# A hand-ordered fast-matrix-product kernel: the third role cast after the next set's second, and the openings and seams put in another order

## The reference

```python
def swiglu(x, w_gate, w_up, w_down):
    return (jax.nn.silu(x @ w_gate) * (x @ w_up)) @ w_down
...
for l in range(2):
    if l == 1: ...                      # shared K, V and log-forget rows from rms_norm(x, g_kv_b)
    x = x + 0.5 * swiglu(rms_norm(x, g_norm[l, 0]), ...)      # D_FF = 2816
    ...                                 # attention, with a cache of 512 rows
    x = x + 0.5 * swiglu(rms_norm(x, g_norm[l, 2]), ...)
y = rms_norm(x, g_final)
```

## Time and profile before

| | us |
|---|---|
| median of 3 runs | 2517.8 (2512.48 to 2520.25) |
| the profiled execution | 2516.2, span 2514.0 |
| PE busy | 2413.0 (96%) |
| DVE busy | 1859.1 (74%) |
| ACT busy | 1338.0 (53%) |
| POOL busy | 546.1 (22%) |
| mean granted TensorE clock | 0.992 of 2.4 GHz |

### The profile page before, as it was taken

One profiled execution on the slowest core, in us unless ns is written; L12 is line 12 of the kernel. 1 busy time (PEld: TensorE's weight loads), 2 busy tenths in 40 slices (PEclk: granted clock), 3 DMA queues, 4 the chain that ended last, 5 costly groups with the idle time before them and its releaser, 6 DMA issues. The chain is left out here.

```text
span 2514.0 us, 48940 instructions
## 1 busy us (share of the span) xinstructions
PE 2413.0 (96%) x18377; PEld 2267.6 (90%) x18377; DVE 1859.1 (74%) x3710; ACT 1338.0 (53%) x2870; POOL 546.1 (22%) x421
## 2 busy tenths in 40 slices
PE   8899999999998999999999999999999999999998
PEld 7899999788678999999988889999996699999998
DVE  7887979422687888787935889787928878787865
ACT  6555556201785655555622555555618856555554
POOL 0222122344000122222135122222131001222210
PEclk9999999999999999999999999999999999999999
DMA  5656565232763465756434665666457644666652
GB/s 133 122 116 139 108 139 105 88 117 85 282 241 108 93 122 112 141 119 133 94 84 138 172 130 111 138 125 129 99 210 255 224 117 78 138 116 138 124 112 82
DMA packets 419397, 334.20 MB, mean 133 GB/s; under 512 B 20641, under 2 KB 379738, under 8 KB 418914
## 3 DMA queue, kind: packets, MB, share of 16 engines
q1 hardware_dynamic: 279376, 246.98, 31.8%
q0 software_dynamic: 133136, 65.82, 21.4%
q10 hardware_dynamic: 6658, 18.37, 2.0%
HBM read 314.98 MB, written 16.13 MB: 132 GB/s over the span
## 5 line engine op out<-in xcount | busy, mean ns | idle before, releaser
L925 PE MATMUL PS<-x_area,w_area 128*128 128x320 f32 x3096 | 482.2, 309 | 0.0
L925 PEld LDWEIGHTS PS<-x_area,w_area 128*128 128x128 f32 x3096 | 461.1, 188 | 0.3 <-DVE w_area L2276 0.3
L2276 DVE TENSOR_TENSOR w_area<-R,w_area 128x512 fp32r<-128x512 f32 (+2 forms) x583 | 357.1, 617 | 119.1 <-ACT w_area L1638 118.3
L1638 ACT ACTIVATE w_area<-R 128x512 fp32r<-128x512 f32 (+2 forms) x583 | 324.8, 567 | 223.3 <-PE PS L925 88.6
L2276 DVE TENSOR_TENSOR r_area<-R,r_area 128x512 fp32r<-128x512 f32 (+2 forms) x437 | 270.6, 620 | 115.4 <-ACT r_area L1638 105.0
L925 PE MATMUL PS<-r_area,w_area 128*128 128x320 f32 x1584 | 271.2, 314 | 25.1 <-ACT PS L1723 17.1
L1638 ACT ACTIVATE r_area<-R 128x512 fp32r<-128x512 f32 (+2 forms) x437 | 248.0, 568 | 60.6 <-DVE R L2297 40.2
L925 PEld LDWEIGHTS PS<-r_area,w_area 128*128 128x128 f32 x1584 | 243.1, 191 | 32.9 <-ACT PS L1723 29.8
L1723 ACT ACTIVATE PS<-PS 128x320 f32<-128x320 f32 x438 | 179.8, 417 | 160.0 <-PE PS L925 143.7
L1148 PE MATMUL PS<-w_area,xn_hi 128*128 128x512 f32 x800 | 252.4, 397 | 4.9 <-POOL w_area L769 3.6
L925 PE MATMUL PS<-r_area 128*128 128x320 f32 x1392 | 238.4, 311 | 8.4 <-ACT PS L1723 6.0
(11 more groups left out here) (341 smaller groups left out, 4169.6 us busy)
## 6 DMA issues: line engine op xcount, KB each, us to landing
R<-in_w_ffn_up_dram SPq DMA_DIRECT2D x45, 512.0 KB, 5.3
R<-in_w_ffn_gate_dram SPq DMA_DIRECT2D x43, 512.0 KB, 5.4
R<-in_w_ffn_up_dram SPq DMA_DIRECT2D x86, 256.0 KB, 3.7
R<-in_w_ffn_up_dram POOLq DMA_DIRECT2D x86, 256.0 KB, 4.7
R<-in_w_ffn_gate_dram SPq DMA_DIRECT2D x82, 256.0 KB, 4.6
R<-in_w_ffn_gate_dram POOLq DMA_DIRECT2D x81, 256.0 KB, 4.9
R<-in_w_ffn_down_dram SPq DMA_DIRECT2D x52, 384.0 KB, 3.8
R<-in_w_ffn_down_dram SPq DMA_DIRECT2D x88, 192.0 KB, 3.2
```

What stands on the lines that cost most here:

```text
L925: last = pe.matmul(PS[:, bank, 0:HT], a[:, k, :], b, start=(start and opens), stop=(k == n - 1 and a is lo), skip_group_check=True)
L1638: act.activation(role_parts(f, g, s, role)[0], role_source(f, g, s, role), ACT.Copy).then_inc(sem("early_cast") if key in EARLY_COUNT else ...
L2276: dve.tensor_tensor(lo, role_source(f, g, s, role), hi.bitcast(F32), ALU.subtract).then_inc(sem("early_split") if key in EARLY_COUNT else ...
```

## The change

1. The third role S3(n) is cast and split after S2(n+1), no longer before S1(n+1): in `splits`, in both engines' `ffn_sets` and in both `opening_down`. PE's order of products stays.
2. In an opening, ACT does copy 1 before the high part of hidden "5" and copy 2 before the high part of S4; PE does each product of the first down set over all its blocks before the next.
3. SP issues S1's quarter of the set after next-but-one ahead of the other transfers of the set before it, which is the new order of the splits.
4. Seams: the first tiles of the projections are loaded as soon as their own raw words are free, the first hidden parts of block 0 and the store of the keys before block 2 come after the first iteration (`after_first`), and one finishing tile moves behind the next projection's first weight tile.

```diff
@@ splits
-        out += ([(then, "W11")] if then else []) + [(at, "S4")] + ([(at, "S3")] if at != order[0] else [])
-        out += ([(then, "S1"), (then, "S2")] if then else []) + [(at, "W22")] + ([(then, "W12")] if then else [])
+        out += ([(then, "W11")] if then else []) + [(at, "S4")] + ([(then, "S1"), (then, "S2")] if then else [])
+        out += ([(at, "S3")] if at != order[0] else []) + [(at, "W22")] + ([(then, "W12")] if then else [])
...
@@ SP, load_ffn
-                for g, s in chain(f):
-                    if set_at(f, g, s) is not early:
-                        quarter_load(f, g, s)
+                sets = [(f, *at) for at in chain(f) if set_at(f, *at) is not early]
+                first_quarter(*sets[0])
+                for key, then in zip(sets, sets[1:] + [None]):
+                    if then is not None:
+                        first_quarter(*then)
+                    other_quarters(*key)
...
@@ SP
             load_ffn(0)
+            load_opening_rows(w_qkv_a[0], "qkv", QKV_ORDER[0])
...
-            sp.wait_ge(stored, STORED["kt"])
+            sp.wait_ge(stored, STORED["bv"])
+            sp.wait_ge(sem("kt_stored"), 16)
...
@@ PE, opening_down
                 product(f, g, s, "W11", "1", q, True)
-                product(f, g, s, "S1", "5", v, True, (), near)
+                product(f, g, s, "S1", "5", v, True)
                 pe.wait_ge(sem("copied"), 3 * i + 1)
-                product(f, g, s, "S2", "6", q, False, (), near)
-                product(f, g, s, "W12", "2", first_rows, False, (), near)
-                product(f, g, s, "S1", "5", v, False, (), last)
-                product(f, g, s, "S2", "6", q, False, (), last)
-                product(f, g, s, "W12", "2", first_rows, False, (), last)
+                product(f, g, s, "S2", "6", q, False)
+                product(f, g, s, "W12", "2", first_rows, False)
                 pe.wait_ge(sem("copied"), 3 * i + 2)
                 product(f, g, s, "S3", "7", q, False)
...
@@ ACT, opening_down
                 hidden_rows(f, *prev, "1")
+                copy_rows(f, *cur, 1)
                 hidden_rows(f, *prev, "5")
-                copy_rows(f, *cur, 1)
                 hidden_rows(f, *prev, "7")
                 hidden_rows(f, *prev, "2")
                 role_high(f, *then, "W11")
+                copy_rows(f, *cur, 2)
                 role_high(f, *cur, "S4")
                 hidden_rows(f, *prev, "4")
+                role_high(f, *then, "S1")
+                role_high(f, *then, "S2")
                 role_high(f, *cur, "S3")
-                role_high(f, *then, "S1")
-                copy_rows(f, *cur, 2)
-                role_high(f, *then, "S2")
                 role_high(f, *cur, "W22")
...
@@ ACT, ffn_sets
                         rows_on(f, *prev, 0)
-                        role_high(f, *cur, "S3")
...
                         role_high(f, *then, "S2")
+                    if n:
+                        role_high(f, *cur, "S3")
                     role_high(f, *cur, "W22")
...
@@ DVE, opening_down
                 hidden_lows(f, *prev, "4")
-                role_low(f, *cur, "S3")
                 dve.wait_ge(w_split, SPLIT[(f, *cur, "S4")])
                 role_sum(f, *then, "S2")
                 role_low(f, *then, "S1")
                 role_low(f, *then, "S2")
                 fifth_rows(f, *cur)
+                role_low(f, *cur, "S3")
                 role_low(f, *cur, "W22")
...
@@ DVE, ffn_sets
                         hidden_sums(f, *prev, ("5", "7", "6"))
-                    if n:
-                        role_low(f, *cur, "S3")
...
                     if turned:
                         hidden_sums(f, *prev, ("4",))
                         hidden_lows(f, *prev, "7")
+                    if n:
+                        role_low(f, *cur, "S3")
                     role_low(f, *cur, "W22")
...
                         hidden_low(f, *prev, 1)
                     if after_gate and not plain:
                         gate_scaled(f, *prev, 1)
+                    if n == 0 and after_first is not None:
+                        after_first()
...
@@ DVE, ffn (the seam into a projection)
                     tile_low(name, 0)
+                    finish_one(KB - 3)
                     sums_out(f, *last)
```

More of the change, by code:

```diff
@@ L635, in load_square @@
                 base, s, first = BASE[name], SLOT[name], 0
-                if free is not None:
+                if free is None:
+                    first = 1
+                    for u in range(2):
+                        opening_tile(name, u, *cols(w, (s + u) % 2, u * P))
+                else:
                     first = 2
@@ L650, in load_square, with opening_tile, row_tile, load_opening_rows @@
                     tile(base + m * 2 + 1, 1 - s, *cols(w, 1 - s, m * 2 * P + P))
-            def load_rows(w, base, par, n_tiles, first=0):
-                with sp.Fori(0, n_tiles) as n:
+            def opening_tile(name, j, view, src):
+                sp.wait_ge(w_split, PLAN.raw_free[name, j])
+                sp.dma_start(view, src).then_inc(w_loaded[LOAD[name, j] % 2], 16)
+            def row_tile(w, s, u, at):
+                return (raw[s][:, 0:1024].rearrange("p (k m) -> p k m", k=2),
+                        w[u * 256:(u + 1) * 256, bass.ds(at, 512)].rearrange("(k p) m -> p k m", p=P))
+            def load_opening_rows(w, name, column):
+                for u in range(4):
+                    opening_tile(name, u, *row_tile(w, (SLOT[name] + u) % 2, u, column * 512))
+            def load_rows(w, base, par, n_tiles, first=0, done=0):
+                with sp.Fori(done, n_tiles) as n:
                     for u in range(4):
                         s = (par + u) % 2
-                        tile(base + n * 4 + u, s, raw[s][:, 0:1024].rearrange("p (k m) -> p k m", k=2),
-                             w[u * 256:(u + 1) * 256, bass.ds(n * 512 + first * 512, 512)].rearrange("(k p) m -> p k m", p=P))
+                        tile(base + n * 4 + u, s, *row_tile(w, s, u, n * 512 + first * 512))
             def load_attention(x, vc, f_scr):
@@ L980, in opening_down @@
             def opening_down(f, g, s):
-                i, n = PLAN.set[f, g, s], depth(g, s)
+                i = PLAN.set[f, g, s]
                 q, v, first_rows = s % 2, 2 + s % 2, 4 + s % 2
-                near, last = range(n - 1), range(n - 1, n)
                 pe.wait_ge(sem("sum_read"), i - 1)
                 product(f, g, s, "W11", "1", q, True)
-                product(f, g, s, "S1", "5", v, True, (), near)
+                product(f, g, s, "S1", "5", v, True)
                 pe.wait_ge(sem("copied"), 3 * i + 1)
-                product(f, g, s, "S2", "6", q, False, (), near)
-                product(f, g, s, "W12", "2", first_rows, False, (), near)
-                product(f, g, s, "S1", "5", v, False, (), last)
-                product(f, g, s, "S2", "6", q, False, (), last)
-                product(f, g, s, "W12", "2", first_rows, False, (), last)
+                product(f, g, s, "S2", "6", q, False)
+                product(f, g, s, "W12", "2", first_rows, False)
                 pe.wait_ge(sem("copied"), 3 * i + 2)
@@ L1842, in ffn_sets, with ffn @@
                         finish_one(tiles)
-                        finish_one(tiles + 1)
+                        if then is not None:
+                            finish_one(tiles + 1)
                 copy_rows(f, *order[-1], 3)
-            def ffn(f, mean=None, finish_one=None, name=None):
-                ffn_sets(f, mean, finish_one)
+            def ffn(f, mean=None, finish_one=None, name=None, after_first=None):
+                ffn_sets(f, mean, finish_one, after_first)
                 if name is not None:
-                    for k in range(2):
-                        tile_high(name, k)
-                        finish_one(KB - 2 + k)
+                    tile_high(name, 0)
+                    finish_one(KB - 3)
+                    tile_high(name, 1)
+                    for k in range(KB - 2, KB):
+                        finish_one(k)
                     return
@@ L2125, in _, with first_hidden_casts @@
             x_highs("4")
-            for part in HIDDEN_PARTS[1:]:
-                first_hidden_cast(part)
-            ffn(0, None, partial(finish_tile, 0, 0, 0, 1), "qkv")
+            def first_hidden_casts():
+                for part in HIDDEN_PARTS[1:]:
+                    first_hidden_cast(part)
+            ffn(0, None, partial(finish_tile, 0, 0, 0, 1), "qkv", first_hidden_casts)
             act.wait_ge(w_used, BASE["qkv"])
@@ L2139, in _ @@
             act.wait_ge(sem("lam_sums"), 2)
-            act.activation(small[:, 4:6], small[:, 6:8], ACT.Exp).then_inc(sem("lam_exps"), 1)
+            act.activation(small[:, 4:6], small[:, 6:8], ACT.Exp).then_inc(sem("small_exps"), 1)
             act.preload_act_table_set("natural_log_exp_and_others")
@@ L2166, in _ @@
             act.wait_ge(step, count.next())
```

(10 more changed lines are left out.)

52 lines of the change are left out of this document (28 added, 24 removed).

## The result

The changed kernel takes 2785.0 us (median of 4 runs, 2782.1 to 2789.6), the kernel before 2518.2: ratio 1.1065, 95% interval 1.1041 to 1.1089. It is slower by 267 us, where 217 were forecast; 2785.04 stands just past the upper end of the range, 2785. The profiled execution has a span of 2780.1 us, 266.1 above the one before.

A forecast was written before the change was run, and what follows sets the result against it. PE, busy 96% of the span, was taken as the bound. Added terms 84 + 43 + 24 + 23 + 1 + 50 - 8 = 217 us on 2516.2 gave 2733, as median 2735 us; eight-in-ten range 2675 to 2785.

The forecast's parts named there:

- 25 turning sets: In turning sets of the four blocks, PE starts S3 3.37 us later each, 84 us in all.
- 15 openings: In each opening, PE starts S3 2.87 us later, at 196.03 instead of 193.16; 43 us in all.
- down sets and the gate sets behind them: Late low S3 in down sets: 24 us at depth 3, 23 at depth 2, and +1 in gate sets after them.
- seams, loads: Block starts and projections: shorter waits for first loads, together -8 us, bounds 0 and -15.
- clock: After 25 + 15 long stalls PE runs slower, 1.4 us each, 56 us, less 6 for four existing falls: 50 us.
- S2's one buffer: Turning sets: S2(n+1) can't be cast before PE ends S2(n), only 3.52 us before PE wants S3(n).
- SP's new order is that of the splits; it adds no transfer: SP's queue of weight loads: the new order adds no transfer; no cost counted for it.
- (c): Gate and up sets: W11's loads become a bound too, 0.35 us in some 88 sets, +31: 2766 us; chance 0.13.
- (a): Whole kernel: the stalls are there but the clock stays up, 50 us less: 2685 us; chance 0.16.
- (b): Turning sets cost only the 1.3 us chain as DVE and ACT run ahead: 131 us more, 2649 us; chance 0.07.
- (d): Third role still in time before W12(n) ends, so only gains count, some 38 us: 2480 us; chance 0.03.
- clock rule weighed in the prediction: PE stalls: only idle gaps above a limit lower the clock; by it alone the sum would lack the 50 us.

The follow-up runs named there:

- e7: Kernel before, with S3(n) in gate and up sets cast and split after S1(n+1) but ahead of S2(n+1): 2513.9 us, ratio 0.9990.
- e5: Changed kernel with SP's order of loads from before, the splits staying new: 2758.9 us, ratio 1.0976 to the kernel before.
- e8: Kernel before with the seams of the change alone; loads, third role and openings as before: 2509.8 us, ratio 0.9983.
- e4: Changed kernel with the store of the keys issued before block 2 again: 2787.7 us, ratio 1.1071 to the kernel before.
- e6: Changed kernel with idle matmuls before S3 in turning sets (12) and openings (14), accumulating into unused columns: 2713.1 us, ratio 1.0796 to the kernel before.

## Why the prediction came out as it did

The terms of the sum, and what stands for each. Idle terms are the differences of PE's waits by place, after less before:

| step | forecast | shown |
|---|---|---|
| 25 turning sets | 84 | 82.5 (3.30 each from start to start; 78.5 as idle) |
| 15 openings | 43 | 41 (66.9 of waits, 26.0 before) |
| down sets and the gate sets behind them | 48 | 42 |
| starts of the four blocks | 0 or less, in the -8 of "seams, loads" | +18.6 |
| all other waits | -8 | -6 |
| clock | 50 | some 82 of PE's 91.8 more busy |

The last line is 91.8 less 10 us of uncovered matmul ends, 0.16 us before each wait, of which there are 160 where there were 96. Of these 10, the turning sets' 82.5 holds 4. With the other 6 the right column is 82.5 + 41 + 42 + 18.6 - 6 + 82 + 6 = 266, the difference of the spans.

**Right.** The place and the size of the stalls, by timing each operation of the two queues in its new order. 171.2 - 164.31 = 6.89 us was the forecast from W22(n-1) to S3, 6.82 came. The opening's S3 2.87 later: 4.35 us of waits in place of 1.57, 2.78. No idle time in up sets. e7 shows that not any move of the third role does it, but the one behind S2. That S2's one buffer is the cause, as the prediction says, is not shown: counted from the buffer alone it had 1.3 us itself, and when the buffer comes free at 180.98, DVE is at the hidden sums and ACT waits for them. Low S3 right behind low S2, ahead of last rows, hidden "4" and low "7", would tell the two apart; no run has it.

**Wrong: the clock, by some 32 us.** The number of long stalls was right, the term was not. Its price, "one stretch at 1.2 in place of 2.4 GHz costs some 1.5 us", was read from 3.49 us at 59.03, of which 0.25 were a wait, and from 3.34 us at 1414.20. For turning sets it comes out: 34 us in 25, where 25 x 1.4 are 35, but as a mean of 5 places that lose nothing and 4 that lose 2.6 to 2.7. For openings it doesn't: all 15 stalls lower the clock, 10 of them at 2.3 to 2.7 us each, and they cost 33 us where 15 x 1.4 are 21. That is 67 us at the 40 places for 56. The other some 15 us are in places that the term counted at nothing, or at -6: block starts and the stalls of 3.1 to 3.8 us in depth-2 sets. How the 15 divide among them isn't measured.

**Wrong: "SP's new order is that of the splits; it adds no transfer", counted at nothing.** It adds no transfer, but in it W11's quarter of a set waits behind S1's quarter of the next, and at a block's start that one waits for the split of S2(0). The block starts took 18.6 us more; 13.6 of them go away with SP's order of before (e5), and e5 puts the whole of that order at 22 to 26 us. The rest of the 18.6 is the third role's and, at block 0, the seams'. The queue of the loads was looked at for steady sets alone, as rival (c). And the step "at block 2 the store of the keys leaves the time of the first weight loads, so most of the 5.8 us should go" is not what happens: with the seams alone the wait is 5.63 us (e8), with the new order of loads 12.6, and 12.9 with the store back (e4). Why the quarter takes 12.9 us to land there (1528.55 to 1541.41), where a gate load has a median of 4.6 us, is settled in part: the DMA engines are full (shares of 1.08, 1.15 and 1.08 from 1524 to 1539). What fills them wasn't taken apart; the store of the keys alone isn't it (e4).

**The rivals.** (a) clock stays up: excluded, 0.956; but e6 is the kernel that it describes, and stands at 2713 where it had 2685. (b) the short chain: excluded, 3.13 to 3.22 us of idle time in all 25. (c) loads as a bound: its price of 31 us is near to the 22 to 26 of e5, but its place is not: no turning set waits for W11's transfer, the block starts do. (d) faster: excluded.

On the clock rule weighed in the prediction: the same stall of 3.13 or 3.14 us (3.22 once) is followed by slow products in 20 of the 25 turning sets and by one at full clock (1.99 us, as at 187.80) in 5. The Trainium skill (TensorE: Matmul & The Clock Gate, section HAM oscillation) ties the fall to a single idle gap above a limit. As the prediction read it, all of them would have stayed at 2.4 GHz, and no single limit on the gap parts the 20 from the 5: the rule does not fit this trace.

## What to carry to other kernels

Before a role, tile or load is moved behind another, look at what that other one waits for and at all that stands between on each engine: one place in the queue (e7, 0.26 us a set) or two (3.3 us a set) makes the whole difference. The same holds for the queue of the loads, and there above all at the start of a block, where no older work covers. Price a stall that lowers the clock from the products behind it, all of them until they are back at their usual length, and test it by filling the stall with idle matmuls.

## What the runs showed of the hardware that wasn't expected

- Idle matmuls in a stall hold the granted clock up. 12 of them, 128 columns each (24 in the profile), took 2.84 us of a stall of 3.14 us, and the mean clock rose from 0.956 to 0.985 or 0.987 with nothing else changed, worth 68 to 72 us in 2785.
- The same stall doesn't always lower the clock: in turning sets 20 of 25 did, in openings (2.53 to 3.55 us) 15 of 15. What tells the five others apart stays open; nothing in the rows around them differs that was found.
